# Two-layer diffusion trunk on one core: an opening without GpSimd custom instructions, window sums by shifted adds, six slots for the first modulation, and a first MLP begun by two tiles and two chunks

## The chip, the cores and the metric

One NeuronCore of a Trainium2 chip. The metric is the device time of one execution in microseconds (us). The engines are PE (TensorE), DVE (VectorE), ACT (ScalarE), POOL (GpSimd) and SP (SyncE), which issues most of the transfers from HBM.

## The reference

One stream of 512 tokens with 1024 features goes through two layers. Each layer is a token mixer and a squared-ReLU MLP, both in RMSNorm before and after, with shift, scale and gate from the conditioning vector `c`. The context stream is not needed for the result at this depth.

```python
silu_c = silu(c)
for i in range(2):
    sh_m, sc_m, gt_m, sh_f, sc_f, gt_f = split(silu_c @ ada_w[i] + ada_b[i], 6)   # 1024 -> 6 x 1024
    h = rms_norm(x, norm_g[i, 0]) * (1 + sc_m) + sh_m
    y = pool_mixer(h, pool_w, pool_scale) if i == 0 else short_conv_mixer(h, conv_in_w, conv_w, conv_out_w)
    x = x + gt_m * rms_norm(y, norm_g[i, 1])
    hf = rms_norm(x, norm_g[i, 2]) * (1 + sc_f) + sh_f
    x = x + gt_f * rms_norm(square(relu(hf @ ffn_w1[i])) @ ffn_w2[i], norm_g[i, 3])
```

`pool_mixer` has four groups of 256 features with windows of 2, 4, 8 and 16 tokens: mean over the window (cut at both ends of the sequence, divided by the true count) less the token itself, times a 256x256 matrix, times `pool_scale`. The conv mixer is 1024 to 3072, a gated convolution over 3 tokens, and 1024 to 1024. The MLP is 1024 to 4096 to 1024.

## The kernel before

Every large product is made of three float32r products of split operands: `w_hi` and `w_lo`, `in_hi` and `in_lo` (or `mid_hi`, `mid_lo`), in `three`, L347 to L350. Weights come in units of 1 MiB (2048 columns on 128 partitions). SP loads unit u into one of two `raw` slots, ACT makes `w_hi` (`split_hi`, L698), DVE makes `w_lo` (`split_lo`, L952), each in one of three slots. A unit is 48 products of 512 columns. Unit 0 holds the pool weights, units 1 to 32 the first MLP, 33 to 48 the conv mixer, 49 to 80 the second MLP. Two units form a pair that fills four PSUM banks; four pairs form a quarter of an MLP, two of them up (`feat_pair`), two down (`tok_pair`).

There is no scheduler. Each engine has its own list of instructions, written out by hand, runs it in order, and waits on semaphores. So whatever stands in an engine's list behind a waiting instruction waits too.

The first modulation (twenty chunks of 256 columns, `PRE`) is computed on PE. `load_pre` (L268) brings a chunk of 1 MiB into one of four slots; it waits until `add_up` has used the slot's last chunk. `add_up` (L509) multiplies it with silu(c) in eight products that share the array in four column groups, each with 32 output rows. `copy_sums` (ACT, L808) copies the partial sums, `turn_up` (PE, L523) adds the four groups and turns them into columns (scale, shift) or into a wide row (gate), and `columns` (DVE, L1129) reads them. Chunks 0 to 7 are scale and shift of the mixer, 8 to 11 its gate, 12 to 19 scale and shift of the MLP.

The opening: ACT and DVE normalize x, PE turns it into features (`turn_x`), ACT copies it to `xn_fm`. Windows of 2 and 4 are made by adds of GpSimd (L1352 to L1362), windows of 8 and 16 by band matrices on PE (`window`, L548), whose tables GpSimd builds with selects. ACT scales the window sums (`mean`, L818), DVE the tokens (`pool_input`), GpSimd subtracts (L1366), ACT and DVE split. `pool_group` (L567) multiplies a group, `group_squares` (ACT) and `group_out` (DVE) read the result, `group_gate` (DVE) applies the gate. `first_x` and `first_norm` (DVE, L1178, L1184) and `first_root` (ACT, L839) make the new x and its norm, a token tile of 128 at a time; `turn_first` (PE, L579), `copy_first` (ACT), `first_input`, `first_hi` and `first_lo` make the input of the MLP, a feature chunk of 128 at a time after all tiles. `start_pairs` (L591) holds the MLP's units 1 to 4, with the chunks 14 to 19 between its products.

Seven later rows of modulation (`LATER_SEGS`) are computed beside the products: DVE adds 56 pieces (`add_ada`, L964), then GpSimd reduces over the partitions (L1405), fetches and broadcasts a norm row (L1342), and DVE finishes (`finish_row`, L1054). The rows are used at two boundaries (`boundary`), between first MLP and conv mixer and between that and the second MLP.

## Time and profile before

| | us |
|---|---|
| median of three runs | 1044.35 (1042.13 to 1045.39) |
| profiled execution, device time | 1042.69 |
| its span in the profile | 1040.9 |
| PE busy | 968.6 (93%) |
| DVE busy | 540.8 (52%) |
| ACT busy | 339.6 (33%) |
| POOL busy | 88.6 (9%) |

Busy time is what an engine's instructions last, and products overlap, so a PE that is busy all the time still has a rate: 0.226 us from one product of 512 columns to the next at full clock. In the timeline a row is one instruction or a run of equal ones; the bracket says how long its engine stood idle before it and on what.

### The profile page before, as it was taken

The numbers are of one execution on the slowest core, as the hardware profiler recorded it, in microseconds if no ns is written. First come the engines' busy times: TensorE is split into PE (matmuls) and PEld (weight loads), VectorE is DVE, ScalarE is ACT, GpSimd is POOL, SyncE is SP. The second block draws the span as 40 slices with busy tenths as digits, with TensorE's granted clock in tenths as the row PEclk, the third lists the DMA queues.
The fourth block names the chain that finished last, engine by engine and source line by source line (L and its number), as shares of the span: only waits on it lengthen the run. The fifth ranks groups of instructions, "written<-read, shape, count | busy, mean of one in ns | idle before, by whom it ended". The sixth has DMA issues, their size and how long they took to land.

```text
span 1040.9 us, 11368 instructions
## 1 busy us (share of the span) xinstructions
PE 968.6 (93%) x4737; PEld 802.0 (77%) x4737; DVE 540.8 (52%) x582; ACT 339.6 (33%) x454; POOL 88.6 (9%) x65
## 2 busy tenths in 40 slices
PE   4685799999999999997999999889999999999997
PEld 3563568888888888887888887688888888888886
DVE  3345247455545645466576766646546433423444
ACT  5345134224214313333333223415213313312332
POOL 2520010003002100200002302000003000000000
PEclk9788889999999999998999999989999999999999
DMA  9547345344353442311555562035342232232301
GB/s 315 172 162 254 109 159 214 134 152 152 124 177 123 144 160 81 120 43 63 184 196 193 200 216 82 6 122 189 129 135 99 90 119 84 82 120 81 119 13 71
DMA packets 78813, 140.29 MB, mean 135 GB/s; under 512 B 3424, under 2 KB 33192, under 8 KB 78763
## 3 DMA queue, kind: packets, MB, share of 16 engines
q1 hardware_dynamic: 78240, 139.48, 39.7%
q8 instruction: 37, 0.61, 0.2%
q14 instruction: 14, 0.11, 0.0%
q0 software_dynamic: 384, 0.05, 0.0%
q10 hardware_dynamic: 138, 0.05, 0.0%
HBM read 137.47 MB, written 2.10 MB: 134 GB/s over the span
## 4 chain that ended last, share of the span: by engine, by line
PE 87%; DVE 3%; ACT 2%; issue 2%; DVEq 0%; ACTq 0%
PE ps L348 28%; PE ps L350 28%; PE ps L349 28%; PE ps L519 1%; ACT w_hi L704 1%; DVE w_lo L954 1%; PE ps L437 1%; ACT work L843 0%; ACT work L836 0%; PE ps L588 0%; PE ps L536 0%; DVE y L1014 0%; DVE in_lo L1025 0%; ACT work L741 0%; ACT in_hi L748 0%
## 5 line engine op out<-in xcount | busy, mean ns | idle before, releaser
L954 DVE TENSOR_TENSOR w_lo<-raw,w_hi 128x2048 fp32r<-128x2048 f32 x81 | 188.3, 2325 | 262.3 <-ACT w_hi L704 262.3
L348 PE MATMUL ps<-in_hi,w_hi 128*128 128x512 f32 (+1 forms) x768 | 292.6, 381 | 29.2 <-DVE in_lo L1199 12.8
L349 PE MATMUL ps<-in_lo,w_hi 128*128 128x512 f32 (+1 forms) x768 | 290.1, 378 | 0.0
L350 PE MATMUL ps<-in_hi,w_lo 128*128 128x512 f32 (+1 forms) x768 | 289.9, 377 | 0.0
L704 ACT ACTIVATE w_hi<-raw 128x2048 fp32r<-128x2048 f32 x81 | 154.6, 1910 | 381.9 <-PE ps L350 381.9
L348 PE MATMUL ps<-w_hi,mid_hi 128*128 128x512 f32 x576 | 224.5, 390 | 1.6 <-DVE w_lo L954 1.6
L350 PE MATMUL ps<-w_hi,mid_lo 128*128 128x512 f32 x576 | 224.1, 389 | 0.0
L349 PE MATMUL ps<-w_lo,mid_hi 128*128 128x512 f32 x576 | 224.1, 389 | 0.0
L348 PEld LDWEIGHTS ps<-in_hi,w_hi 128*128 128x128 f32 x768 | 148.9, 194 | 58.7 <-issue 17.3
L350 PEld LDWEIGHTS ps<-in_hi,w_lo 128*128 128x128 f32 x768 | 148.9, 194 | 25.5
L349 PEld LDWEIGHTS ps<-in_lo,w_hi 128*128 128x128 f32 x768 | 149.2, 194 | 24.8
L348 PEld LDWEIGHTS ps<-w_hi,mid_hi 128*128 128x128 f32 x576 | 108.1, 188 | 24.2 <-DVE w_lo L954 2.1
L350 PEld LDWEIGHTS ps<-w_hi,mid_lo 128*128 128x128 f32 x576 | 108.1, 188 | 22.5
L349 PEld LDWEIGHTS ps<-w_lo,mid_hi 128*128 128x128 f32 x576 | 108.1, 188 | 22.3
L964 DVE SCALAR_TENSOR_TENSOR ada_sum<-ada_raw,silu_t,ada_sum 128x1024 f32<-128x1024 f32 x56 | 74.9, 1338 | 1.3
L972 DVE TENSOR_TENSOR work<-work 128x512 f32<-128x512 f32 x64 | 44.1, 689 | 38.1 <-ACT mid_hi L715 37.8
L713 ACT ACTIVATE work<-ps 128x512 f32<-128x512 f32 x64 | 38.2, 598 | 75.9 <-DVE mid_lo L974 39.3
L983 DVE TENSOR_TENSOR y<-y,ps 128x512 f32<-128x512 f32 x48 | 32.2, 684 | 47.0 <-PE ps L350 47.0
L974 DVE TENSOR_TENSOR mid_lo<-work,mid_hi 128x512 fp32r<-128x512 f32 x64 | 49.3, 771 | 2.2
L1405 POOL PARTITION_ALL_REDUCE gate_row<-ada_sum x3 | 18.7, 6240 | 363.7 <-DVE ada_sum L964 363.7
L1405 POOL PARTITION_ALL_REDUCE mod_rows<-ada_sum x4 | 24.5, 6114 | 219.4 <-DVE ada_sum L964 219.4
L715 ACT ACTIVATE mid_hi<-work 128x512 fp32r<-128x512 f32 x64 | 40.5, 632 | 2.0
(137 smaller groups left out, 512.0 us busy)
## 6 DMA issues: line engine op xcount, KB each, us to landing
raw<-in_ffn_w_dram SPq DMA_DIRECT2D x64, 1024.0 KB, 5.2
ada_raw<-in_ada_w_dram SPq DMA_DIRECT2D x56, 512.0 KB, 5.6
raw<-in_conv_in_w_dram SPq DMA_DIRECT2D x16, 512.0 KB, 5.1
ada_raw<-in_ada_w_dram SPq DMA_DIRECT2D x6, 1024.0 KB, 6.0
ada_sum<-in_ada_w_dram SPq DMA_DIRECT2D x6, 1024.0 KB, 6.3
mod_rows<-in_ada_w_dram SPq DMA_DIRECT2D x5, 1024.0 KB, 7.8
raw<-in_conv_in_w_dram SPq DMA_DIRECT2D x4, 1024.0 KB, 5.9
raw<-in_conv_out_w_dram SPq DMA_DIRECT2D x4, 1024.0 KB, 6.0
```

Of the source, the lines that this page charges most:

```text
L348: nc.tensor.matmul(o, hi, b_hi, start=start, stop=False)
L349: nc.tensor.matmul(o, hi, b_lo, start=False, stop=False)
L350: return nc.tensor.matmul(o, lo, b_hi, start=False, stop=stop)
L704: nc.scalar.activation(w_hi[:, u % W_SLOTS, :], raw[:, u % RAW_SLOTS, :], ACT.Copy).then_inc(w_hi_ready, 1)
L713: nc.scalar.activation(work[:, n % 2, :], bank(p, m), ACT.Relu).then_inc(relu_done, 1)
L715: nc.scalar.activation(mid_hi[:, n, :], work[:, n % 2, :], ACT.Square).then_inc(hid_hi, 1)
L954: nc.vector.tensor_tensor(w_lo[:, u % W_SLOTS, :], raw[:, u % RAW_SLOTS, :], w_hi[:, u % W_SLOTS, :].bitcast(F32), ALU.subtract).then_inc( ...
L964: nc.vector.scalar_tensor_tensor(out=ada_sum[:, s % 2, :], in0=ada_raw[:, i % ADA_SLOTS, :], scalar=silu_t[:, 3, k:k + 1], in1=ada_sum[:, ...
L972: nc.vector.tensor_tensor(work[:, n % 2, :], work[:, n % 2, :], work[:, n % 2, :], ALU.mult).then_inc(hid_sq, 1)
L974: nc.vector.tensor_tensor(mid_lo[:, n, :], work[:, n % 2, :], mid_hi[:, n, :].bitcast(F32), ALU.subtract).then_inc(hid_lo, 1)
L983: nc.vector.tensor_tensor(y_tok[:, t, half(h)], y_tok[:, t, half(h)], bank(p, t), ALU.add).then_inc(y_sum, 1)
L1405: nc.gpsimd.partition_all_reduce(to, ada_sum[:, s % 2, :], channels=P, reduce_op=bass.bass_isa.ReduceOp.add).then_inc(row_summed, 1)
```

## The change

It replaces the opening and the way of the seven rows. No custom instruction of GpSimd is left (`partition_broadcast`, `partition_all_reduce`).

- Pool scale and the norm row are spread over the partitions by a one-row product on PE (`spread`), and DVE copies them. The gate's bias enters `add_up` as a one-row product, and DVE's `gate_copy` multiplies the sums with the norm row, so `group_out` leaves; ACT copies the group behind its squares.
- Windows are shifted sums over a padded `xn_fm`: window 2 on DVE, windows 4, 8 and 16 on GpSimd, with a product for the cut ends. The bands leave PE, `mean` leaves ACT, `pool_input` moves to ACT, scaling and subtraction become one DVE instruction (`diff`).
- Chunks 0 and 1 get slots of their own in `y`, so six chunks are asked for at once. The pairs use banks 0, 1, 4, 5 and 2, 3, 6, 7. The load of unit 1 stands before those of chunks 12 to 19.
- GpSimd makes `w_lo` of units 1, 2 and 3.
- The MLP's input for chunks 0 to 3 is made in quarters of two tiles and two chunks, straight from PSUM; unit 1 is multiplied in these quarters, then half of unit 2, unit 3, the rest of unit 2, unit 4.
- A later row is summed by four products on PE between two units of a pair (`sum_row`), finished by DVE from PSUM, written to DRAM and read back to all partitions. Its pieces are added at units `LATER_AT`.

```diff
+PRE_SLOTS = [4, 5] + [(i - 2) % 4 if i < PRE_F else 1 + (i - PRE_F + 1) % 3 for i in range(2, len(PRE))]
+LATER_AT = [4 + i for i in range(24)] + [28, 28, 29, 29, 30, 30, 35, 35] + [36 + i // 2 for i in range(16)] + [52 + i for i in range(8)]
+ROW_AT = {LATER_AT[NC * s + NC - 1] + 1: s for s in range(len(LATER_SEGS))}
+BANKS = ((0, 1, 4, 5), (2, 3, 6, 7))
...
             load(POOL_U)
-            for i in range(2, PRE_F + 2):
+            for i in range(2, PRE_F):
                 load_pre(i)
-            for u in range(1, 4):
-                load(u)
-                load_pre(PRE_F + 2 * u)
-                load_pre(PRE_F + 2 * u + 1)
+            load(1)
+            for i in range(PRE_F, PRE_F + 4):
+                load_pre(i)
+            load(2)
+            for i in range(PRE_F + 4, PRE_F + 6):
+                load_pre(i)
+            load(3)
+            for i in range(PRE_F + 6, len(PRE)):
+                load_pre(i)
...
+            def sum_row(u, p, free):
+                s = ROW_AT[u]
+                pe.wait_ge(ada_used, NC * (s + 1))
+                free(3)
+                for j in range(4):
+                    mm = nc.tensor.matmul(bank(p + 1, 3)[32 * j:32 * (j + 1), 0:Q], ones[:, 0:32], ada_sum[:, s % 2, quarter(j)],
+                                          start=True, stop=True)
+                mm.then_inc(row_summed, 1)
...
                 last.then_inc(unit_done, 1)
                 need_weights(u + 1)
+                if u + 1 in ROW_AT:
+                    sum_row(u + 1, p, next_free)
...
+            def spread(row):
+                for e in range(2):
+                    mm = nc.tensor.matmul(ps[:, e, :], ones[0:1, :], row[0:1, half(e)], start=True, stop=True)
+                mm.then_inc(row_spread, 1)
...
+                turn_first(0, 0)
+                turn_first(0, 2)
+                turn_first(1, 0)
+                part(0, 0)
+                add_up(PRE_F + 2)
+                turn_first(0, 3)
+                add_up(PRE_F + 3)
+                turn_first(1, 2)
+                turn_up(PRE_F + 2)
+                turn_up(PRE_F + 3)
+                turn_first(0, 1)
+                turn_first(1, 3)
+                part(1, 0)
+                turn_first(1, 1)
+                add_up(PRE_F + 4)
+                part(0, 1)
+                turn_up(PRE_F + 4)
+                part(1, 1).then_inc(unit_done, 1)
+                add_up(PRE_F + 5)
+                pe.wait_ge(f_made, 4)
+                second_unit(2)
...
+            pe.wait_ge(ones_ready, 1)
+            pe.wait_ge(row_in, 16 * 3)
+            spread(pool_row)
+            pe.wait_ge(ident_ready, 1)
...
             for i in range(4):
                 add_up(i)
-                window(BAND_CHUNK + i)
                 turn_up(i)
-            add_up(4)
+            pe.wait_ge(row_wide, 2)
             need_weights(POOL_U)
-            pool_group(0)
...
+            for g in range(1, GROUPS):
+                add_up(2 * g + 2)
+                pool_group(g - 1)
+                turn_up(2 * g + 2)
+                add_up(2 * g + 3)
+                turn_up(2 * g + 3)
             pool_group(3)
+            for i in range(10, PRE_F + 2):
+                add_up(i)
+                turn_up(i)
...
+            def diff(n):
+                dve.wait_ge(pool_h, n + 1)
+                dve.wait_ge(mod_step, n // 2 + 1)
...
+                nc.vector.scalar_tensor_tensor(out=win[:, n, :], in0=win[:, n, :], scalar=A_BY_W[:, n:n + 1], in1=xn_in[:, n, :],
+                                               op0=ALU.mult, op1=ALU.subtract).then_inc(pool_diff, 1)
...
+            def add_windows(g):
+                w, n = WINDOWS[g], slice(2 * g, 2 * g + 2)
+                length = T + w - 2
+                at = PAD - w // 2
+                nc.gpsimd.tensor_tensor(sums[0][:, :, 0:length], xn_fm[:, n, at:at + length], xn_fm[:, n, at + 1:at + 1 + length], ALU.add).then_inc(pairs_read, 1)
+                pool.wait_ge(pairs_read, g)
+                shift, level = 2, 0
+                while shift < w:
...
+                    nc.gpsimd.tensor_tensor(o, src[:, :, 0:length], src[:, :, shift:shift + length], ALU.add).then_inc(sum_step, 1)
...
+            for u in (1, 2, 3):
+                pool.wait_ge(w_hi_ready, u + 1)
+                pool.wait_ge(w_lo_ready, u)
+                nc.gpsimd.tensor_tensor(w_lo[:, u % W_SLOTS, :], raw[:, u % RAW_SLOTS, :], w_hi[:, u % W_SLOTS, :].bitcast(F32), ALU.subtract).then_inc(w_lo_ready, 1)
...
-                nc.gpsimd.partition_all_reduce(to, ada_sum[:, s % 2, :], channels=P, reduce_op=bass.bass_isa.ReduceOp.add).then_inc(row_summed, 1)
...
+                pool.wait_ge(row_made, s + 1)
+                pool.dma_start(rows_dram[s].rearrange("(j n) -> j n", j=4), fin[0:P:32, :]).then_inc(row_out, 16)
```

On ACT, `split_hi(1)` now stands before `first_root(0)`, `split_hi(2)` behind `first_hi(3)`, `split_hi(3)` behind `copy_sums(18)`. On DVE the columns of chunk 12 stand before `first_norm(0)`, those of chunk 13 before `first_x(3)`.

## Rows read from the trace of the kernel before

**Rows 1.** Stretches: bounds, length, PE, PEld, DVE, ACT, POOL busy, PEclk, DMA share, GB/s

```profile
106.10:171.50 65.40, 58.68 (x296) 44.46 (x297) 29.50 (x41) 22.80 (x30) 3.81 (x6) 0.90 0.42 142
171.50:474.00 302.50, 302.50 (x1340) 250.57 (x1339) 159.78 (x152) 89.53 (x101) 26.93 (x13) 1.00 0.38 130
...
96.00:102.00 6.00, 2.85 (x32) 1.94 (x30) 1.13 (x4) 4.54 (x6) 0.00 (x0) 1.00 1.03 358
```

**Rows 2.** Timeline of PE: start, duration, line, operation, and idle before it

```profile
42.16 1.01 PE L536 MATMUL ps<-picks,cu 128*128 128x1 f32 x4 [6.31 <-ACT cu L812]
...
48.55 0.58 PE L348 MATMUL ps<-w_hi,in_hi 128*128 128x256 f32 x1 [3.52 <-DVE w_lo L954]
...
53.83 0.75 PE L536 MATMUL ps<-picks,cu 128*128 128x1 f32 x4
...
56.09 0.61 PE L536 MATMUL ps<-picks,cu 128*128 128x1 f32 x4 [0.50 <-ACT cu L812]
56.56 0.36 PE L348 MATMUL ps<-w_hi,in_hi 128*128 128x256 f32 x1
...
59.60 1.07 PE L519 MATMUL ps<-ada_sum,cu 128*32 128x256 f32 x16
...
71.15 0.69 PE L533 MATMUL ps<-gate_row,ones 1*128 1x256 f32 x2
...
106.14 0.77 PE L348 MATMUL ps<-in_hi,w_hi 128*128 128x512 f32 x1 [6.17 <-DVE in_lo L1199]
...
119.42 0.79 PE L348 MATMUL ps<-in_hi,w_hi 128*128 128x512 f32 x1 [4.19 <-DVE in_lo L1199]
...
171.52 0.39 PE L348 MATMUL ps<-w_hi,mid_hi 128*128 128x512 f32 x1
...
641.58 0.50 PE L348 MATMUL ps<-w_hi,mid_hi 128*128 128x512 f32 x1 [1.64 <-DVE w_lo L954]
```

**Rows 3.** Timeline of POOL

```profile
13.12 0.28 POOL L1327 TENSOR_SCALAR_AFFINE_SELECT ident<-ident 128x128 f32<-128x128 f32 x1 [11.26 <-issue]
...
22.59 1.30 POOL L1342 PARTITION_BROADCAST pool_row<-pool_row  x1 [7.12 <-issue]
...
32.79 1.88 POOL L1352 TENSOR_TENSOR win<-xn_fm 128x1022 f32<-128x1022 f32 x1 [7.71 <-issue]
...
46.95 3.92 POOL L1366 TENSOR_TENSOR win<-win,xn_fm 128x512 f32<-128x512 f32 x2 [3.73 <-ACT win L826]
...
634.85 6.11 POOL L1405 PARTITION_ALL_REDUCE mod_rows<-ada_sum  x1 [35.47 <-DVE ada_sum L964]
```

**Rows 4.** Timeline of DVE

```profile
24.01 3.14 DVE L1205 TENSOR_TENSOR raw<-raw,pool_row 128x1024 f32<-128x1024 f32 x2 [4.40 <-POOL pool_row L1342]
...
85.21 2.48 DVE L1181 SCALAR_TENSOR_TENSOR xs<-y,st,xs 128x1024 f32<-128x1024 f32 x2
...
636.55 4.98 DVE L954 TENSOR_TENSOR w_lo<-raw,w_hi 128x2048 fp32r<-128x2048 f32 x1 [1.80 <-ACT w_hi L704]
```

**Rows 5.** Timeline of ACT

```profile
44.27 1.90 ACT L704 ACTIVATE w_hi<-raw 128x2048 fp32r<-128x2048 f32 x1
...
91.05 1.02 ACT L850 ACTIVATE xn_tok<-ps 128x1024 f32<-128x1024 f32 x1 [1.68 <-PE ps L588]
```

**Rows 6.** Chain that ended last, one piece: start, duration, what

```profile
71.50 1.46 ACT work L836 x8
```

**Rows 7.** Costliest groups of the page: count, busy, mean ns of one, idle before

```profile
L954 DVE TENSOR_TENSOR w_lo<-raw,w_hi 128x2048 fp32r<-128x2048 f32 x81 | 188.3, 2325 | 262.3 <-ACT w_hi L704 262.3
...
L964 DVE SCALAR_TENSOR_TENSOR ada_sum<-ada_raw,silu_t,ada_sum 128x1024 f32<-128x1024 f32 x56 | 74.9, 1338 | 1.3
```

**Rows 8.** DMA issues of the page: count, KB each, median us to landing

```profile
ada_sum<-in_ada_w_dram SPq DMA_DIRECT2D x6, 1024.0 KB, 6.3
mod_rows<-in_ada_w_dram SPq DMA_DIRECT2D x5, 1024.0 KB, 7.8
```

More of the change, by code:

```diff
@@ L600, in products @@
-                def products(u, k, m, chunk, start, stop):
-                    pe.wait_ge(f_lo, chunk + 1)
-                    o = feat_products(u, k, m, 0 if u in (1, 3) else 1, chunk, COLS, ALL, start, stop)
-                    if (u, k, m) in later:
-                        later[u, k, m]()
-                    return o
-                add_up(PRE_F + 2)
-                need_weights(1)
-                for k in range(UK):
-                    for m in range(4):
-                        last = products(1, k, m, k, k == 0, False)
@@ L612, in start_pairs, with part @@
[L612 to L622 removed]
+                def part(side, pair):
+                    pe.wait_ge(f_lo, FIRST_MADE.index((side, pair)) + 1)
+                    need_weights(1)
+                    for k in (2 * pair, 2 * pair + 1):
+                        for m in range(4):
+                            last = feat_products(1, k, m, 0, k, COLS, toks(2 * side, 2), k == 0 and side == 0, False)
+                    return last
@@ L623, in start_pairs @@
                 pe.wait_ge(cols_read, cols_value(len(PRE) - 1))
-                for k in range(UK):
-                    for m in range(2, 4):
-                        last = products(2, k, m, k, k == 0, False)
-                last.then_inc(unit_done, 1)
+                second_unit(0)
+                second_unit(1).then_inc(unit_done, 1)
                 need_weights(4)
@@ L882, in _ @@
             copy_sums(7)
-            mean(6)
-            mean(7)
-            copy_sums(8)
+            pool_input(6)
+            pool_input(7)
             diff_hi(6)
@@ new lines, in _ @@
+            nc.gpsimd.memset(xn_fm[:, :, 0:PAD], 0.0)
+            nc.gpsimd.memset(xn_fm[:, :, PAD + T:], 0.0).then_inc(pads_ready, 1)
+            for g in range(1, GROUPS):
+                for at, tokens in edges(g):
+                    for i, (_, count) in enumerate(tokens):
+                        op = nc.gpsimd.memset(edge[:, at + i:at + i + 1], WINDOWS[g] / count)
+            op.then_inc(edge_ready, 1)
+            pool.wait_ge(xn_copied, NT)
+            pool.wait_ge(pads_ready, 1)
```

572 lines of the change are left out of this document (265 added, 307 removed).

## The prediction

> **What bounds the kernel now.** I began with the busy shares by slice: PE is at 9 tenths nearly everywhere and falls only in the first four slices and at two later places. The table of stretches [rows 1] shows it in numbers. From 171.5 to 474 us PE is busy 302.5 of 302.5 us at full clock, one product each 0.226 us, so nothing that this change does to other engines can shorten that stretch. Before it the last stretch of the opening, 106.1 to 171.5, has PE busy 58.7 of 65.4 us at 0.90 of the clock. So I take the opening as a chain, see where each link waits, and rebuild the chain with the new orders. The end of it is one event: the first product of the MLP's second half, at 171.52 us [rows 2]; behind it the code of the PE stream is the same but for seven small sums. The change is worth what this event moves, less what the later part gains or loses.
>
> **Where the opening waits today.** GpSimd switches what it can run: it stands 11.26 us before the first select, 7.12 before the first broadcast, 7.71 before the first add of a window [rows 3]. The last add is done at 39.7; ACT has `mean(0)` in its queue ahead of `copy_sums(3)`, so PE stands 6.31 us at 42.16 [rows 2]; then w_hi and w_lo of the pool weights, and the first pool product comes at 48.55 [rows 2]. The pool stage then needs 36.7 us to `first_x(0)` at 85.21 [rows 4], the way from there to the MLP's first product 20.9 us (to 106.14), and the first four MLP units 65.4 us.
>
> **Step A, to the first pool product: 48.55 becomes 37.** The select at 13.12 and so the transposes at 13.63 stay. xn of tile 1 is now ready before ident, so the four turns run with only ACT's copies (1.0 us each, as the copy of a tile in [rows 5]) between them, and the features are complete at about 20.3 instead of 22.0. The spread of a row by PE is new: 256 columns of such a one-row product take 0.69 us at 71.15 [rows 2], so the four pieces of a row make at most 2.8, and I take 2.5, as they overlap; the first lies under the wait for ident, the second ends at 21.3. The 7.12 and 7.71 us before a broadcast and after it I take as gone with the broadcast; between 0 and 7.7 us may still stand before the adds, and the cover below hides either. The DVE then has: row copy 1.2 and two-window add 1.3 (nearest: 1.24 for 1024 elements, 2.48 for two [rows 4]), `columns` 0.5 twice, which come at 25.7 because the chunks follow each other each 2.1 us (add_up 1.07 at 59.60, ACT's copy 0.50 and turn_up 0.61 at 56.09 [rows 2]); the pool weights 3.1 (L1205 [rows 4]) to 28.8; two diffs 1.4 (half of 1.24 each and a little); ACT's hi, hi and w_hi, at 1.90 for 2048 elements [rows 5] 0.6+0.6+1.9, to 32.8; w_lo 2.3 [rows 7] to 35.1; add_up(4), 1.07 or cold 1.93, to about 37. Gain 11.5. The window sums on GpSimd: an add costs 1.88 us for 1022 elements [rows 3], there are 2+3+4 of these and five short ones of about 0.2, so 18.7 us from 20.5: group 1 is ready at 25 and needed at 37, group 2 at 31.5 and needed at 48, group 3 at 40 and needed at 56. That is the cover that hides a switch or a slow GpSimd.
>
> **Step B, pool stage: 36.7 becomes 34.5.** Four pool groups: the first cold 5.3 (48.55 to 53.83 [rows 2]), three warm at 3.0 (24 products; 56.56 to 59.60) = 14.3. Three plain add_ups 3.2, four with the bias product 1.07+0.35 = 5.7; eight turn_ups 5.0; the bias product is half of the 0.69 at 71.15, being in one of four column groups (bounds 0 and 0.69, 1.4 either way); ACT copies that nothing covers, five at 0.5 = 2.5; twice ACT's squares and the new copy of the group (1.46 [rows 6] and 1.02 [rows 5]) stand ahead of the sum copy, 1.1 each = 2.2; last gate product 1.2, at the same rate, and a short reciprocal on DVE = 1.4. Sum 34.3, so `first_x(0)` starts at about 71.5 instead of 85.2. The copy and the squares lie on ACT beside PE's next group; in the group where ACT is late they cost the 1.1 counted. One to three more cold groups would cost 2.3 each (5.3 less 3.0).
>
> **Step C, to the first MLP product: 20.9 becomes 13.8.** DMA is what counts: load(1) is issued once add_up(10) is done, 66.2, ahead of the slots of chunks 12 and 13. A loaded queue moves 358 GB/s [rows 1], 2.93 us for 1 MiB; the first lands after 5.7, for the 6.3 of [rows 8] held some queueing: 71.9, 74.9, 77.8. add_up(13), copy, turn_up, `columns` (1.1+0.5+0.6+0.4) bring DVE to 80.4; first_x(3) 1.28; ACT's squares and root 1.5; first_norm(3) 0.9; one turn 0.6, first_lo(0) 0.75. Together 85.3, against 106.14. `first_input(0)`, `first_norm(2)` and w_hi of unit 1 lie beside. Unit 1's w_lo is now GpSimd's: 2048 elements at 1.84 ns are 3.8 us, done at 77.6; cover until 85.
>
> **Step D, the first four units: 65.4 becomes 61.6.** Unit 1 in halves, 96 products of 256 columns at 0.12, the spacing in a warm pool group [rows 2], = 11.5; units 2 to 4, 144 at 0.2265 = 32.6; six add_ups 6.4; six turn_ups 3.0; five turns of the first tiles 3.0; half clock at the start 1.4 (the first product after a stall takes 0.77 or 0.79 instead of 0.39 [rows 2], and a few more like it); a bare copy 0.5; unit 2's w_lo late by 1.1 and unit 3's by 2.1, because ACT's w_hi comes only behind `first_hi(3)` and `copy_sums(18)` and GpSimd needs 3.8 where DVE needs 2.3. Sum 61.6: PE reaches the MLP's second half at 146.9. Today's stretch holds 43.5 us of products, 9.5 of chunks and 12 of waits; of the waits, 4.19 at 119.42 [rows 2] and a smaller one go, because two tiles and two chunks are ready while the rest is made. The opening gains 24.6.
>
> **Step E, the seven later rows.** GpSimd's reduce (6.11 us [rows 3]) and broadcast leave; PE gets four products of 256 columns. The eight of an add_up take 1.07 us [rows 2], so about 0.55 each row, 3.9 us in all; bounds 0.3 and 1.1 each, 2 to 8. It waits for `ada_used`. At the start of unit u (odd, second last of a pair) DVE still has about 2.1 us of hidden work, ACT 1.3 and then w_hi 1.9, then DVE w_lo 2.3 and one ada product 1.34 [rows 7] or two: done 6.9 to 8.3 us on, while the sum stands 10.9 us on (48 x 0.2265). So the margin is 2.6 to 4 us and the wait costs nothing; without it, the products of the pair's second unit would stand behind it. The round trip through DRAM has more than ten microseconds of cover, as the row is wanted units later. DVE's finish shrinks, off the path.
>
> **Step F, the second boundary.** The reduce at 634.85 runs to 640.96, and beside it w_lo takes DVE 4.98 us instead of 2.3 [rows 3, 4, 7]; PE stands 1.64 us behind it at 641.58 [rows 2]. That wait goes: -1.6. The boundary's other waits are chains of ACT and DVE that no edit touches. Ada products beside steps 28 to 30 delay the first boundary by nothing: DVE waits there for the second product group in any case.
>
> **A rule that speaks against it.** Beside DVE's two-operand work GpSimd's two adds of 512 took 3.92 us, alone 0.94 each would be 1.9 [rows 3]. The Trainium skill, "GPSIMD Engine Reference", section Key points, says that GpSimd shares its SBUF interfaces with VectorE and that an instruction of DVE with two SBUF inputs contends with it; by that rule the trace agrees, and what it does here is rival 1. The same page, section 3.1, gives 4.5 us for an add of 2048 elements and calls DVE twice as fast; no add of that length is in the trace, my 3.8 is scaled from 1022 elements, and by the page's figure unit 2 and unit 3 would each come 0.7 us later, 1022 becoming 1023.4.
>
> **The sum.** 1042.69 - 24.6 + 3.9 - 1.6 = 1020.4 for an execution like the profiled one (span 1040.9 and 1.8 around it). The median of the three runs shown is 1.7 above it, so 1022.
>
> **Rivals.** (1) GpSimd becomes the bound. With the factor 2.1 of [rows 3] the window sums last 39 us, end at 60 and are needed at 56, +4; the w_lo of units 2 and 3 come 4.1 later each; with one more cold group about 14: 1036. For it: DVE is busy over half of the opening. Against: DVE idles just where units 2 and 3 are split. Chance 0.14. (2) The loads come later than reckoned: 1 MiB took 6.3 us in the median from issue to landing in one slot and 7.8 in another [rows 8], and load(1) is put before chunks 12 and 13. If these overlap badly, chunk 13 lands at 86 instead of 77.8, +8: 1030. For it: the queue of 12 MiB behind 66 us; against: 358 GB/s were held over whole stretches. Chance 0.12. (3) Better than reckoned: no cold group, the waits in D all covered, 5.3 less 3.0, 1.4 and 3.2: 1015. Chance 0.10. (4) Slower: PE now waits in its own stream for DVE's ada products. If these stand one unit (10.9 us) further back in DVE's queue than I count, each sum waits 10.9 less a margin of 2.6 to 4, so about 7.5 us seven times, 53 us, against a gain of 22: 1075. It decides from 3.2 us a row on. Against: DVE is busy 53% from 171.5 to 474. Chance 0.03. (5) The opening isn't shorter, since its chain is bound by something I don't see, as ACT's order, and only E and F remain: 1042.69 + 3.9 - 1.6 + 1.7 = 1047. Chance 0.03.
>
> **Chances and range.** The forecast itself has 0.58, with 1017 to 1028 as its own range. From 1013 to 1036 it reaches into rivals 1 to 3 and holds 0.8 or a little more. Faster by over 0.3% (3 us, about what a measurement tells from nothing) is the forecast with rivals 1 to 3, 0.94; same 0.02; slower 0.04.
>
> **What would show it.** First pool product near 37, `first_x(0)` near 71.5, first MLP product near 85, the MLP's second half near 147. GpSimd's adds start at about 20.5 with no long idle. Its w_lo of 2048 takes 3.8 us; 8 would be rival 1. No PE wait at the seven sums. It is wrong if PE's second half of the MLP starts later than 158 or if products between 147 and 450 show waits.

## The result, and the profile after

The changed kernel takes 1035.26 us (median of 4 runs, 1034.93 to 1036.25) against 1044.43 before (median of 4): a ratio of 0.9917 [0.9899, 0.9934], so 9.2 us faster. The forecast was 1022. The profiled execution took 1035.34 us with a span of 1033.6.

PE is busy 970.5 us, GpSimd 69.2 instead of 88.6. The page of the kernel after, the lines by slices (25.8 us each, busy share in tenths, PEclk the granted clock):

```profile
PE 970.5 (94%) x4769; PEld 797.7 (77%) x4769; DVE 538.7 (52%) x563; ACT 339.8 (33%) x448; POOL 69.2 (7%) x103
PE   6486999999999999997999999799999999999997
PEclk9596999999999999998999999989999999999999
```

The second slice (25.8 to 51.7 us) still has PE at 4 tenths; there the forecast failed. The timeline of PE after, with the milestones that answer to [rows 2] (start, duration, operation, idle before it and its cause):

```profile
8.66 3.75 PE L595 MATMUL ps<-pool_row,ones 1*128 1x512 f32 x4 [8.66 <-DMA gate_row<-in_ada_b_dram]
...
37.57 1.02 PE L589 MATMUL ps<-picks,cu 128*128 128x1 f32 x4 [6.54 <-ACT cu L870]
...
45.98 1.93 PE L574 MATMUL ps<-ada_sum,cu 128*32 128x256 f32 x16 [7.40 <-issue]
47.84 0.58 PE L380 MATMUL ps<-w_parts,in_hi 128*128 128x256 f32 x1
...
84.93 1.93 PE L574 MATMUL ps<-ada_sum,cu 128*32 128x256 f32 x16 [4.49 <-DMA ada_sum<-in_ada_w_dram]
...
96.61 0.56 PE L380 MATMUL ps<-in_hi,w_parts 128*128 128x256 f32 x1
...
131.30 0.70 PE L380 MATMUL ps<-in_hi,w_parts 128*128 128x512 f32 x1 [2.74 <-POOL w_parts L1425]
...
160.25 0.39 PE L380 MATMUL ps<-w_parts,mid_hi 128*128 128x512 f32 x1
...
236.18 0.39 PE L382 MATMUL ps<-in_hi,w_parts 128*128 128x512 f32 x1
236.50 0.64 PE L409 MATMUL ps<-ada_sum,ones 128*32 128x256 f32 x8
237.07 0.50 PE L380 MATMUL ps<-in_hi,w_parts 128*128 128x512 f32 x1
...
237.63 0.39 PE L382 MATMUL ps<-in_hi,w_parts 128*128 128x512 f32 x1
```

| milestone | before [rows 2, 4] | forecast | after |
|---|---|---|---|
| first pool product | 48.55 | 37 | 47.84 |
| `first_x(0)` starts on DVE | 85.21 | 71.5 | 81.83 |
| first MLP product | 106.14 | 85.3 | 96.61 |
| MLP's second half | 171.52 | 146.9 | 160.25 |
| from there to the end of the span | 869.4 | 871.7 | 873.3 |

Of the 13.4 us by which 160.25 misses 146.9, 10.8 are there at the first pool product. The two rows 37.57 and 45.98 show where: PE stands 6.54 us on ACT's copy of a chunk and then 7.40 for which the profile names nothing ("issue"). In the kernel the wait for the split pool weights (`need_weights(POOL_U)`) stands right ahead of this chunk, and DVE's `w_lo` (41.46, 4.42 us) ends at 45.88; so this wait, too, is for DVE. ACT in its turn waits for DVE. The table of stretches says who is busy (length, PE, PEld, DVE, ACT, POOL, granted clock, share of DMA, GB/s):

```profile
20.00:46.00 26.00, 10.41 (x87) 5.33 (x86) 24.39 (x18) 6.63 (x10) 24.70 (x15) 0.61 0.65 208
46.00:82.00 36.00, 29.78 (x256) 21.17 (x256) 16.44 (x32) 20.01 (x54) 0.14 (x1) 0.90 0.48 158
```

In the 26 us before the first pool product DVE is busy 24.4 and GpSimd 24.7. Neither has that much to do: in the second experiment below DVE's same operations from the pool weights to `w_lo` take 8.6 us instead of 19.9. The two timelines after, first GpSimd's:

```profile
20.59 1.90 POOL L1403 TENSOR_TENSOR sums<-xn_fm 128x1028 f32<-128x1028 f32 x1 [17.97 <-ACT xn_fm L863]
22.57 2.93 POOL L1410 TENSOR_TENSOR win<-sums 128x1024 f32<-128x1024 f32 x1
...
27.88 2.77 POOL L1410 TENSOR_TENSOR sums<-sums 128x1032 f32<-128x1032 f32 x1
...
36.73 4.26 POOL L1410 TENSOR_TENSOR sums<-sums 128x1048 f32<-128x1048 f32 x2
...
113.31 4.61 POOL L1425 TENSOR_TENSOR w_parts<-raw,w_parts 128x2048 fp32r<-128x2048 f32 x1 [24.61 <-ACT w_parts L761]
```

and DVE's:

```profile
21.40 1.23 DVE L1159 COPY ada_raw<-ps 128x1024 f32<-128x1024 f32 x1 [4.42 <-PE ps L595]
22.54 1.22 DVE L1176 TENSOR_TENSOR win<-xn_fm 128x1024 f32<-128x1024 f32 x1
23.79 1.74 DVE L1178 TENSOR_SCALAR win<-win 128x2 f32<-128x2 f32 x1
...
25.62 0.17 DVE L1197 SCALAR_TENSOR_TENSOR mod<-mod,vec 128x2 f32<-128x2 f32 x1
...
26.01 5.72 DVE L1271 TENSOR_TENSOR raw<-raw,pool_row 128x1024 f32<-128x1024 f32 x2
31.65 3.04 DVE L1211 SCALAR_TENSOR_TENSOR win<-win,mod,xn_fm 128x512 f32<-128x512 f32 x2
...
34.80 1.87 DVE L1197 SCALAR_TENSOR_TENSOR mod<-mod,vec 128x2 f32<-128x2 f32 x1
...
36.78 4.75 DVE L1216 SCALAR_TENSOR_TENSOR in_lo<-win,mod,in_hi 128x512 fp32r<-128x512 f32 x2
41.46 4.42 DVE L1003 TENSOR_TENSOR w_parts<-raw,w_parts 128x2048 fp32r<-128x2048 f32 x1
...
115.13 2.81 DVE L1197 SCALAR_TENSOR_TENSOR mod<-mod,vec 128x2 f32<-128x2 f32 x1
```

An operation of DVE on 2 elements (L1178) takes 1.74 us here; one like it at 25.62 takes 0.17. It starts at 23.79 and is over at 25.53, when GpSimd's add that began at 22.57 is over (25.50). L1197 at 115.13, again 2 elements, lasts 2.81 us, to 117.94; GpSimd's `w_lo` beside it runs from 113.31 to 117.92. In the other direction, GpSimd's add at 22.57 took 2.93 us instead of 1.90: DVE's two-window add had begun at 22.54 and was over at 23.76. So the reading is that an instruction that one of the two has begun keeps the other out to its end. DVE's copy out of PSUM at 21.40 took 1.23 beside an add that kept its 1.90, so an operation that reads from PSUM alone isn't held. The reading is made on GpSimd's adds and subtractions. Beside the custom reduce of the kernel before (634.85 to 640.96, [rows 3]) `w_lo` was over at 641.53 [rows 4], only 0.57 us behind it and with 2.29 of its own, so there it wasn't kept out to the end.

Work held in DVE from 26 to 46 us, each less its time alone (2.36, 1.41, 0.16, 1.41 and 2.29 in the rows of the second experiment): 3.36 + 1.63 + 1.71 + 3.34 + 2.13 = 12.2 us. DVE has no idle time between these rows, and PE's chunk and first pool product follow them. (In the second experiment, where the hold-up is gone from here, DVE waits 0.80 us for ACT instead, and 11.4 of the 12.2 are won.)

The Trainium skill, "SBUF — State Buffer", section Who interferes with whom, describes just this: the port pair that VectorE and GpSimd share is locked for a whole instruction and not split, against an instruction of VectorE with two SBUF inputs, or one in a two-port mode, and the one that issues later blocks. The ends that coincide (117.94 and 117.92) agree with it. The prediction drew only on the short sentence of the GpSimd page.

The effect stood in the trace of the kernel before as well. An operation on 2 elements like the one that takes 0.16 at 27.25 there took 1.05 beside GpSimd's two subtractions (40.73, 2.49 us for two). DVE's timeline before:

```profile
40.96 1.05 DVE L1146 SCALAR_TENSOR_TENSOR mod<-mod,vec 128x2 f32<-128x2 f32 x1
```

### The profile page after: what moved, and what is told of

It reads as the page before. It is cut to its first block, busy times and chain, and to the rows that moved or that the text cites. A ratio compares the mean times of both kernels' runs of the same rounds, so it can differ in the third digit from the quotient of the medians.

```text
span 1033.6 us, 11447 instructions
## 1 busy us (share of the span) xinstructions
PE 970.5 (94%) x4769; PEld 797.7 (77%) x4769; DVE 538.7 (52%) x563; ACT 339.8 (33%) x448; POOL 69.2 (7%) x103
## 3 DMA queue, kind: packets, MB, share of 16 engines
HBM read 141.77 MB, written 2.13 MB: 139 GB/s over the span
## 4 chain that ended last, share of the span: by engine, by line
PE 88%; DVE 2%; ACT 1%; issue 1%; DMA 1%; POOL 0%; DVEq 0%; SPq 0%; ACTq 0%
PE ps L380 29%; PE ps L381 28%; PE ps L382 28%; PE ps L574 1%; DMA ada_sum<-in_ada_w_dram 1%; PE ps L488 1%; ACT w_parts L761 1%; POOL w_parts L1425 0%; PE ps L589 0%; PE ps L409 0%; PE ps L632 0%; DVE xn_tok L1257 0%; DVE y L1063 0%; DVE in_lo L1074 0%; ACT work L798 0%
## 5 line engine op out<-in xcount | busy, mean ns | idle before, releaser
L1003 DVE TENSOR_TENSOR w_parts<-raw,w_parts 128x2048 fp32r<-128x2048 f32 x78 | 180.8, 2320 | 265.6 <-ACT w_parts L761 265.5
L380 PE MATMUL ps<-in_hi,w_parts 128*128 128x512 f32 (+1 forms) x784 | 295.3, 377 | 19.7 <-issue 7.8
L381 PE MATMUL ps<-in_lo,w_parts 128*128 128x512 f32 (+1 forms) x784 | 292.8, 373 | 0.0
L382 PE MATMUL ps<-in_hi,w_parts 128*128 128x512 f32 (+1 forms) x784 | 292.5, 373 | 0.0
L761 ACT ACTIVATE w_parts<-raw 128x2048 fp32r<-128x2048 f32 x81 | 154.6, 1910 | 391.4 <-PE ps L382 389.8
L380 PE MATMUL ps<-w_parts,mid_hi 128*128 128x512 f32 x576 | 224.4, 390 | 0.0
L382 PE MATMUL ps<-w_parts,mid_lo 128*128 128x512 f32 x576 | 224.1, 389 | 0.0
L381 PE MATMUL ps<-w_parts,mid_hi 128*128 128x512 f32 x576 | 224.1, 389 | 0.0
L380 PEld LDWEIGHTS ps<-in_hi,w_parts 128*128 128x128 f32 x784 | 152.3, 194 | 49.9 <-issue 12.3
L382 PEld LDWEIGHTS ps<-in_hi,w_parts 128*128 128x128 f32 x784 | 152.3, 194 | 24.6
L381 PEld LDWEIGHTS ps<-in_lo,w_parts 128*128 128x128 f32 x784 | 152.5, 195 | 24.1
L380 PEld LDWEIGHTS ps<-w_parts,mid_hi 128*128 128x128 f32 x576 | 108.1, 188 | 22.4
L382 PEld LDWEIGHTS ps<-w_parts,mid_lo 128*128 128x128 f32 x576 | 108.1, 188 | 22.4
L381 PEld LDWEIGHTS ps<-w_parts,mid_hi 128*128 128x128 f32 x576 | 108.1, 188 | 22.3
L1021 DVE TENSOR_TENSOR work<-work 128x512 f32<-128x512 f32 x64 | 44.1, 689 | 45.6 <-ACT mid_hi L772 45.4
L589 PEld LDWEIGHTS ps<-picks,cu 128*128 128x128 f32 x64 | 10.1, 223 | 18.7 <-ACT cu L870 18.5
```

The lines of the kernel that those rows point to most:

```text
L380: nc.tensor.matmul(o, hi, b_hi, start=start, stop=False)
L381: nc.tensor.matmul(o, hi, b_lo, start=False, stop=False)
L382: return nc.tensor.matmul(o, lo, b_hi, start=False, stop=stop)
L761: nc.scalar.activation(w_hi[:, u % W_SLOTS, :], raw[:, u % RAW_SLOTS, :], ACT.Copy).then_inc(w_hi_ready, 1)
L1003: nc.vector.tensor_tensor(w_lo[:, u % W_SLOTS, :], raw[:, u % RAW_SLOTS, :], w_hi[:, u % W_SLOTS, :].bitcast(F32), ALU.subtract).then_inc( ...
L1021: nc.vector.tensor_tensor(work[:, n % 2, :], work[:, n % 2, :], work[:, n % 2, :], ALU.mult).then_inc(hid_sq, 1)
```

## The experiments

Theory 1 is that the hold-up of DVE and GpSimd eats the gain of the opening. Its rivals are the order of PE's and DVE's work (the spread of the rows ahead of the turns) and the loads. All runs stood beside runs of the kernel before, whose medians were 1043.57 to 1043.90 us (1044.43 beside the kernel after). So a difference of 1 us between a run here and the kernel after means nothing by itself, and the ratios to before are the better measure.

One more rival is the rate of PE, which differs between executions (last experiment). It does not explain step A: in the traces of after, e1, e2 and e9 the first spread takes the same 3.75 us, `add_up(0)` starts at 21.29, 21.04, 21.23 and 20.81, and of the five chunks up to the first pool product the first takes 1.07 us and the last three 1.93 in all four (1.94 in e9), the second 1.07 or, in e1, 1.63.

**e1: GpSimd's sums nearly empty.** One full add for each group stays; the window sums of 4, 8 and 16 are not computed.

```diff
-                    o = win[:, n, :] if 2 * shift == w else sums[(level + 1) % 2][:, :, 0:length]
-                    nc.gpsimd.tensor_tensor(o, src[:, :, 0:length], src[:, :, shift:shift + length], ALU.add).then_inc(sum_step, 1)
+                    nc.gpsimd.tensor_tensor(sums[(level + 1) % 2][:, :, 0:2], src[:, :, 0:2], src[:, :, shift:shift + 2], ALU.add).then_inc(sum_step, 1)
```

> Changed kernel, but GpSimd makes one full add per window group (3 of 1.9 us) and tiny ones else, so the window sums of 4, 8 and 16 tokens are left out of the computation. Theory 1 (GpSimd's adds and DVE's work between 20 and 46 us hold each other up; DVE took 5.72 us for the pool weights where it took 3.14 before, 4.75 for two diff_lo where 1.41 is seen later, 4.42 for w_lo where 2.29): DVE's instructions fall back to 2.45, 1.4 and 2.3 once the adds end at about 27, the first pool product comes at 38 to 40 instead of 47.8, first_x(0) at 72 to 75 instead of 81.8, the kernel takes 1025 to 1028 us. Theory 2 (the chain is bound by the landing of chunk 4 or by ACT's order): the first pool product stays at 47 to 48 and the time at 1035.

Measured: 1026.66 us (1026.13 to 1027.76), ratio 0.9838 [0.9821, 0.9854], first pool product at 37.98. Theory 1 had 38 to 40 and 1025 to 1028. The hold-up isn't wholly gone: one full add for each group is left, and DVE's `in_lo` at 30.69 took 3.12 us instead of 1.41. GpSimd's timeline of this kernel has the effect at its purest:

```profile
20.35 0.29 POOL L1403 TENSOR_TENSOR sums<-xn_fm 128x64 f32<-128x64 f32 x1 [17.73 <-ACT xn_fm L863]
...
26.73 2.20 POOL L1411 TENSOR_TENSOR sums<-sums 128x4 f32<-128x4 f32 x2
```

A sum of 64 elements took 0.29 us, and two sums of 4 elements took 2.20: they lie beside DVE's product of the pool weights (26.40, 2.47 us for two).

**e2: all the work, but two groups' sums behind the split of the pool weights.** The result is whole.

```diff
             for g in range(1, GROUPS):
+                if g == 2:
+                    pool.wait_ge(w_lo_ready, 1)
                 add_windows(g)
```

> Changed kernel with all its work; GpSimd only waits for w_lo of the pool weights before it begins windows 8 and 16. Theory 1: after about 26 us DVE is alone, w_lo is ready at about 37, the first pool product at 38 to 40; then windows 8 and 16 run from 37 to about 55 beside the first two pool groups, in DVE's idle time, and are needed at about 46 and 56; part of the gain may be given back there. Time 1025 to 1030 us. Theory 2: first pool product at 47 to 48, and window 8 then late besides, so 1035 to 1040.

Measured: 1032.37 us (1028.42 to 1033.07), ratio 0.9883 [0.9863, 0.9904]; first pool product at 36.48, `first_x(0)` at 74.89. DVE's timeline of this kernel shows its operations alone, and then the hold-up again where the sums now lie:

```profile
25.95 2.36 DVE L1271 TENSOR_TENSOR raw<-raw,pool_row 128x1024 f32<-128x1024 f32 x2
28.23 1.41 DVE L1211 SCALAR_TENSOR_TENSOR win<-win,mod,xn_fm 128x512 f32<-128x512 f32 x2
...
29.74 0.16 DVE L1197 SCALAR_TENSOR_TENSOR mod<-mod,vec 128x2 f32<-128x2 f32 x1
...
30.02 1.41 DVE L1216 SCALAR_TENSOR_TENSOR in_lo<-win,mod,in_hi 128x512 fp32r<-128x512 f32 x2
32.23 2.29 DVE L1003 TENSOR_TENSOR w_parts<-raw,w_parts 128x2048 fp32r<-128x2048 f32 x1 [0.80 <-ACT w_parts L761]
...
35.52 3.85 DVE L1211 SCALAR_TENSOR_TENSOR win<-win,mod,xn_fm 128x512 f32<-128x512 f32 x2 [0.93 <-ACT xn_fm L881]
...
41.61 1.88 DVE L1201 TENSOR_SCALAR mod<-mod 128x2 f32<-128x2 f32 x1
```

The first five rows are the times alone; 35.52 and 41.61 are held (3.85 and 1.88 us instead of 1.41 and, for 2 elements, 0.17), now behind the first pool product. 11.4 us are won there and 6.9 at `first_x(0)`: 4.5 go back in the pool stage, where PE now waits for DVE's `in_lo` (1.27 us at 46.53) and longer for ACT (2.81 at 55.08 instead of 1.51). The first product came earlier than theory 1 had it (38 to 40), the median time later (1025 to 1030). The traced execution, 1028.42, is the fastest; the other three took 1032.27 to 1033.07, so by the median only 2.9 us are gained on after, and where those three lost 4 us isn't traced.

**e9: the same adds, each in two halves.** The diff shows the first add of a group; the others are halved likewise. The same bytes, so a shared bandwidth would change nothing; a lock for whole instructions would.

```diff
-                nc.gpsimd.tensor_tensor(sums[0][:, :, 0:length], xn_fm[:, n, at:at + length], xn_fm[:, n, at + 1:at + 1 + length], ALU.add).then_inc(pairs_read, 1)
+                for e in (0, 1):
+                    op = nc.gpsimd.tensor_tensor(sums[0][:, e, 0:length], xn_fm[:, 2 * g + e, at:at + length], xn_fm[:, 2 * g + e, at + 1:at + 1 + length], ALU.add)
+                op.then_inc(pairs_read, 1)
```

> The changed kernel with each of GpSimd's full adds (1.9 us for 2 x 512) issued as two adds of 512, the same work in all. The ends of DVE's slowed operations fall on the ends of GpSimd's adds (DVE on 2 elements: 115.13 + 2.81 = 117.94, GpSimd's w_lo: 113.31 + 4.61 = 117.92). Theory A, the two engines exclude each other by whole instructions: an operation of DVE that reads its operands from SBUF waits for the end of the instruction that GpSimd has begun, and the reverse. Then each of DVE's eight held operations between 26 and 46 us waits for one half add, some 0.95 us instead of 1.5 to 1.9: 5 to 6 us of the 12 go, the first pool product moves from 47.84 to 42 to 43.5, the time to 1030 to 1032 if GpSimd's later end costs nothing. Theory B, they share bandwidth, each at half speed while both work: the same bytes, the first pool product stays at 47 to 48.5 and the time at 1035 to 1036.5.

Measured: 1030.14 us (1027.83 to 1030.61), ratio 0.9864 [0.9844, 0.9884], first pool product at 39.75. DVE's timeline of this kernel:

```profile
23.31 0.89 DVE L1178 TENSOR_SCALAR win<-win 128x2 f32<-128x2 f32 x1
...
25.40 3.25 DVE L1271 TENSOR_TENSOR raw<-raw,pool_row 128x1024 f32<-128x1024 f32 x2
...
31.66 0.82 DVE L1197 SCALAR_TENSOR_TENSOR mod<-mod,vec 128x2 f32<-128x2 f32 x1
...
35.50 2.28 DVE L1003 TENSOR_TENSOR w_parts<-raw,w_parts 128x2048 fp32r<-128x2048 f32 x1
```

2 elements take 0.89 and 0.82 us instead of 1.74 and 1.87, the weights 3.25 instead of 5.72, the split 2.28 instead of 4.42. Theory B falls: 5.1 us of the median for no work less. The product came even earlier than the 42 to 43.5 of theory A. Not each operation gained alike: held over their time alone, the weights are 0.89 us, the two diffs 1.57 (2.98 in all, hardly less than the 3.04 after), the 2 elements 0.66, `in_lo` 1.57 (2.98), and the split not at all: GpSimd then had only its two short operations for the cut ends of the windows (35.11, 2.73 us for two on 8 elements), and they waited for the split. Together 4.7 us instead of 12.2, so 7.5 of the 8.1; another 0.5 is the earlier start (`add_up(0)` at 20.81).

**e4: PE turns the first two tiles before it spreads the pool's scale.**

```diff
-            pe.wait_ge(row_in, 16 * 3)
-            spread(pool_row)
...
             for j in range(NT):
+                if j == 2:
+                    pe.wait_ge(row_in, 16 * 3)
+                    spread(pool_row)
                 turn_x(j)
...
             norm_x(0)
-            row_on_all(0, pool_row[:, :])
...
             norm_x(3)
+            row_on_all(0, pool_row[:, :])
```

DVE's copy of the spread row goes behind its four tiles with it.

> Changed kernel, but PE turns tiles 0 and 1 before it spreads the pool scale. PE stood until 8.7 us for the row's transfer and then needed 3.75 us at half clock, while xn of tile 0 was ready at 9.3 and ident at 1.6. Theory A: features complete near 17 instead of 20.5, the whole opening moves by 2.5 to 3.5 us, time 1032. Rival B (the start is bound by the transfers of x and the first chunks): under 1 us, 1034.5 to 1035.5.

Measured: 1033.44 us (1032.15 to 1038.27), ratio 0.9912 [0.9891, 0.9932]; `add_up(0)` at 18.37 (after: 21.29), first pool product at 44.93. The spread at 8.66 in the timeline after was a cost of 2 to 3 us that step A had put under a wait for `ident`; `ident` was there at 1.6 us. The traced execution is 2.6 us ahead at the MLP's second half (157.67); the median falls by 1.8, between the two theories, and by the ratios it isn't told from after.

**e3: the loads of chunks 12 and 13 ahead of unit 1's.**

```diff
-            for i in range(2, PRE_F):
+            for i in range(2, PRE_F + 2):
                 load_pre(i)
             load(1)
-            for i in range(PRE_F, PRE_F + 4):
+            for i in range(PRE_F + 2, PRE_F + 4):
```

> Changed kernel, but the loads of chunks 12 and 13 are asked for before that of unit 1. Theory A (PE stands 4.5 us at add_up(12) and works at half clock after it, since chunk 12 is queued behind unit 1, whose load waits for add_up(10)): the wait goes, add_up(12) starts near 80.5 instead of 84.9, first MLP product near 92 instead of 96.9, time 1030 to 1032. Rival B (the wait is only moved: unit 1 lands later, its w_lo on GpSimd becomes the last): first MLP product at 95 to 97, time 1034 to 1036.

Measured: 1035.64 us (1034.58 to 1036.96), ratio 0.9921 [0.9906, 0.9936]; the first MLP product at 96.66 against 96.61. PE's timeline, then ACT's, of this kernel:

```profile
85.48 1.01 PE L589 MATMUL ps<-picks,cu 128*128 128x1 f32 x4 [3.75 <-ACT cu L870]
```

```profile
81.88 1.91 ACT L761 ACTIVATE w_parts<-raw 128x2048 fp32r<-128x2048 f32 x1 [1.30 <-DMA raw<-in_ffn_w_dram]
...
85.06 0.36 ACT L870 ACTIVATE cu<-ps 128x256 f32<-128x256 f32 x1
```

The wait of 4.49 us for the load (84.93 after) became 3.75 for ACT's copy of the chunk: in ACT's order the split of unit 1 (81.88) stands ahead of it, and that one now waits for its load. Product and time are where rival B put them, but not for its reason: the first MLP product has no wait before it, so `w_lo` of unit 1 wasn't the last.

**e5 and e6: e2 and e4 together, and then the loads with ACT's order mended.** e6 also has the loads of e3, and ACT's split of unit 1 stands behind the copy of chunk 12 and the root of tile 1:

```diff
-            split_hi(1)
             first_root(0)
             copy_sums(PRE_F)
             first_root(1)
+            split_hi(1)
```

> The two changes of e2 and e4 together: GpSimd's sums of windows 8 and 16 wait for the split of the pool weights, and PE turns the first two token tiles before it spreads the pool's scale. Theory A, the two act on different links of one chain (e2: DVE's work between add_up(0) and the first pool product; e4: the start of add_up(0)), so their gains add: add_up(0) at 18.4 us, first pool product at 33.5 to 34.5 (e2 had 36.48), and the time 2 to 3 us under e2's median of 1032.4, 1029.5 to 1030.5. Theory B, behind e2 another thing (the loads of chunks, the sums of windows 8 and 16 that now end at 52 us) sets the pace: first pool product earlier but first_x(0) at 74 to 75 as in e2, time 1031.5 to 1033.

> As e5, and the loads of chunks 12 and 13 ahead of the load of unit 1, with ACT's split of unit 1 behind the copies of chunk 12 and the root of tile 1, so that it no longer stands ahead of them. Theory A: the wait of 4.3 to 4.6 us for chunk 12 goes, and the split of unit 1 (ACT 1.9, GpSimd 4.5 after the load) is still in time: first MLP product 3 to 4 us nearer to first_x(0) than in e2 (14.6 there), 11 to 12, and the time 3 us under e5. Theory B: unit 1 becomes the last thing ready (its load now lands some 5 us later, at about 80, and 6.4 us of splitting follow), the wait is at the first MLP product instead and the time is within 1 us of e5.

Measured: e5 1028.56 us (1025.21 to 1037.38), ratio 0.9868 [0.9833, 0.9903], first pool product at 33.41 and `first_x(0)` at 71.78, so up to there theory A: the gains add. The runs are 12 us apart, so the median can't tell its 1029.5 to 1030.5 from the 1031.5 to 1033 of theory B. e6 1032.51 us (1026.14 to 1037.64), ratio 0.9896 [0.9871, 0.9921]: no gain, and neither theory's picture. In e6 the turn of chunk 12 still waited 3.50 us for ACT's copy and the next turns 3.91 for DVE. From `first_x(0)` to the first MLP product it is 14.7 us in e5 and 16.2 in e6, where theory A had 11 to 12; which one thing sets this stretch is not settled.

**e7: `w_lo` of units 2 and 3 on DVE again.**

```diff
-            for u in (1, 2, 3):
+            for u in (1,):
                 pool.wait_ge(w_hi_ready, u + 1)
...
             first_lo(3)
+            split_lo(2)
...
             first_lo(4)
+            split_lo(3)
```

> The w_lo of units 2 and 3 on DVE (as before the change) instead of GpSimd; unit 1's stays on GpSimd. PE waited 2.74 us at 131.3 behind GpSimd's w_lo of unit 3, and beside GpSimd's two a DVE operation on 2 elements took 2.81 instead of 0.16 us. Theory A, that wait is worth its length: MLP's second half 2.5 to 3 us earlier (157.5), time 1032.3 to 1033. Theory B, DVE's own chain (first_input, first_lo) slips by its 2.3 us and PE waits there instead: time 1035 to 1036.

Measured: 1032.25 us (1031.86 to 1032.56), ratio 0.9888 [0.9872, 0.9904]. PE's timeline of this kernel:

```profile
129.21 0.50 PE L380 MATMUL ps<-in_hi,w_parts 128*128 128x512 f32 x1 [0.49 <-DVE w_parts L1003]
```

Where PE stood 2.74 us (131.30 after) it stands 0.49, and the median falls by 3.0. The MLP's second half begins at 156.54 instead of 160.25, from a first MLP product at nearly the same time (96.46, 96.61). Theory A.

**e8: each row sum twice.**

```diff
-                for j in range(4):
+                for j in (0, 1, 2, 3) * 2:
```

> The four products that sum a row over the partitions are issued twice, seven times in the kernel. The stream of PE shows a set as 0.64 us and the products behind it 0.77 us later than without. Theory A, the price is the products' own rate: seven more sets cost 7 x 0.64 to 0.77 = 4.5 to 5.4 us, 1039.7 to 1040.7. Theory B, most of it is a fixed cost of entering and leaving the four column groups: a second set adds 0.43 or less each, 3 us or less, 1036.5 to 1038.3.

Measured: 1038.87 us (1037.61 to 1039.56), ratio 0.9951 [0.9937, 0.9964]: 3.6 us more than after. PE's timeline of this kernel, the doubled set:

```profile
236.78 1.07 PE L409 MATMUL ps<-ada_sum,ones 128*32 128x256 f32 x16
237.78 0.50 PE L380 MATMUL ps<-in_hi,w_parts 128*128 128x512 f32 x1
```

A set is 0.64 us, two are 1.07: 0.43 for the products. In the stream after, 236.18 to 237.63 is 1.45 us where three steps of 0.227 make 0.68: 0.77 more. So 0.43 is products and 0.34 is paid once for a set. That it is the going in and out of the four column groups is not shown: PE's waits for `ada_used` and for the bank stand ahead of the first set alone, and could be it. Seven more sets at 0.43 are 3.0 of the measured 3.6; theory B is the nearer, by the stream (0.44 more from the product before the sum to the one after it, at each of the seven places) rather than by the time, whose interval reaches both theories.

**e10, e11, e12: the edits that gained, together.** e10 is e2 with e7, e11 is e5 with e7, e12 is e11 with GpSimd's adds in halves.

> e2 and e7 together: the sums of windows 8 and 16 behind the split of the pool weights, the w_lo of units 2 and 3 on DVE. They act on different stretches, so theory A adds them: e2's median 1032.4 less 3.0 = 1029.4. Theory B, in e7 the gain came from where the loads fell, and with the opening 6 us earlier they are late instead: 1031 to 1032.5. As for the spread of the runs: e2, e4 and e5 had runs 4 to 12 us apart and e7 within 0.7; if the early opening itself spreads them (loads racing the chain), e10 spreads by 4 us or more; if only the moved turns do (e4, e5), by 4 us at most as e2.

> e5 and e7 together, the three edits that each gained. Additive: e5's 1028.6 less 3.0 = 1025.6, the lowest run near 1022.2. Rival: DVE is the engine that ends last after e5, so its 4.6 us more of w_lo show: 1027 to 1029.

> e11 with GpSimd's adds in halves. Theory A (exclusion by whole instructions): DVE's operations beside the sums of windows 8 and 16, at 35 to 50 us, wait for halves; in e2 they took 3.85, 3.08 and 4.14 us instead of 1.4 and 1.88 instead of 0.17, so up to 4 us of 9 go, of which some lies under PE's products of a pool group: 1 to 3 us under e11. Theory B (shared bandwidth): as e11 within 1 us.

| | median us | runs | ratio to before |
|---|---|---|---|
| e10 | 1025.13 | 1020.49 to 1029.55 | 0.9815 [0.9788, 0.9842] |
| e11 | 1025.22 | 1022.00 to 1031.37 | 0.9827 [0.9791, 0.9864] |
| e12 | 1021.48 | 1018.32 to 1027.35 | 0.9792 [0.9763, 0.9821] |

e12, with the whole result, beats both kernels: 22.4 us under before and 13.8 under after. It is 3.7 us under e11, where theory A had 1 to 3, but the intervals of the two overlap and the traced e11 had the slower PE in its opening (below), so this doesn't count as a second proof beside e9. e11 came where the additive sum had it (1025.6). e10 came out 4.3 us under its additive 1029.4, below both of its theories, and is no slower than e11, which has one more gaining edit; so the gains aren't simply additive. The medians of these kernels are uncertain by some 3 us, for their runs spread by 9.

Why some of them spread, one comparison suggests. e5 and e11 have the same instructions up to the first pool product. PE's timeline of e5, then of e11:

```profile
12.44 1.98 PE L595 MATMUL ps<-pool_row,ones 1*128 1x512 f32 x4
...
18.15 1.07 PE L574 MATMUL ps<-y,cu 128*32 128x256 f32 x16
...
33.41 0.58 PE L380 MATMUL ps<-w_parts,in_hi 128*128 128x256 f32 x1
```

```profile
12.70 3.78 PE L595 MATMUL ps<-pool_row,ones 1*128 1x512 f32 x4
...
23.72 1.94 PE L574 MATMUL ps<-y,cu 128*32 128x256 f32 x16
...
41.21 0.58 PE L380 MATMUL ps<-w_parts,in_hi 128*128 128x256 f32 x1
```

The same spread takes 1.98 us in one and 3.78 in the other, the same chunk 1.07 and 1.94, and the first pool product differs by 7.8 us. The granted clock is given as 1.00 from 9 to 20 us in both; the rate of the products is what differs, by a factor of nearly two. From 20 to 33 us the record says 0.59 in e5 and 1.00 in e11, and yet a chunk takes 1.93 us in both (25.97 in e5, 27.11 in e11). So the clock on record can't be read before its first change; the length of a known row can. The kernel after, too, begins at the lower rate (3.75 for the spread at 8.66, 1.98 for the one at 19.38); in e11 it goes on to the first pool product. What decides isn't settled.

e11's runs fall in two heaps, 1022.0 to 1022.3 and 1028.2 (the profiled one) to 1031.4, with a mean clock on record of 0.968 to 0.969 in the first and 0.976 in the second: the slower have the higher one, as they would if they, too, had the lower rate under a clock given as 1.00. Of the slower three one is traced. It isn't the whole of the spread. e10, which leaves PE's turns where they were, spreads by 9 us as well, and there the higher clock goes with the shorter time (0.973 at 1020.49, 0.965 at 1029.55); its expectation had put 4 us or more down to the early opening itself.

## Why the prediction was wrong

It missed by 1035.34 less 1020.4, 14.9 us for an execution like the profiled one. Step by step:

- **Step A, 37 forecast, 47.84 measured (10.8 of the 14.9). This step failed.** Its terms for DVE, the pool weights 3.1, two diffs 1.4 and `w_lo` 2.3, took DVE's times without a GpSimd beside it, and the 18.7 us of adds on GpSimd were laid beside them, with a cover of 12 to 16 us. The cover held: neither PE nor DVE nor ACT has a row from 20 to 82 us that waits for GpSimd. But beside them DVE was held for 12.2 us, and DVE was the chain: from the columns to the end of `w_lo` 9.4 us were forecast (25.7 to 35.1) and 19.9 measured (26.01 to 45.88). e1 takes most of the adds away and gets 37.98; e2 moves them and gets 36.48 with all the work done; e9 halves their length and gets 39.75. Rival 1 had the contention and its factor [rows 3], but charged it to GpSimd alone, and so priced the wrong engine. The trace could have told: beside GpSimd's work `w_lo` took 4.98 instead of 2.3 us [rows 4, 7], which the prediction itself used in step F, and 2 elements took 1.05 (40.96 above).
- **Within step A**, the select and the start were too late (`ident` at 1.6 instead of 13.4, no 11.26 us wait at all) and the spread of the pool's scale too cheap (3.75 us, and 8.66 us of waiting for its row, where 2.5 and a cover were taken). The two errors cancelled by luck: `add_up(0)` came at 21.29, as forecast, and e4 shows 2.9 us to be had there.
- **Step B** 34.5 forecast, 34.0 measured.
- **Step C** 13.8 forecast, 14.8 measured. The loads were on time, so rival 2 did not come: chunk 12's products began 3.1 us after `first_x(0)` (forecast 3.4 for its landing), chunk 13's 6.5 after it (6.3). But PE stood 4.49 us before them, and its clock was low (0.59 in the row below): a chunk took 1.93 us and its turn 1.01 where the sum had 1.1 and 0.6. The table of stretches after:

```profile
80.00:100.00 20.00, 12.38 (x70) 8.81 (x70) 13.17 (x23) 10.16 (x19) 4.79 (x1) 0.59 1.02 334
```

- **Step D** 61.6 forecast, 63.6 measured. PE's waits came as forecast, 0.69, 0.51 and 2.74, 3.9 together against 3.2 and 0.5. The chunks and turns took 11.2 us instead of 12.4. What was short is the term for half clock, 1.4: the products of the four units took 48.5 us from start to start where 44.1 and this 1.4 were reckoned, 3.0 more, at a mean granted clock of 0.94 (the first of them 0.56 instead of 0.28 us). The wait of 2.74 is what e7 takes away, and with it some of the low clock: its products took 47.2. GpSimd's `w_lo` took 4.79, 4.61 and 4.50 us where 3.8 was reckoned from a shorter add. The Trainium skill, "GPSIMD Engine Reference", section 3.1, has 4.5 us for 2048 elements; the rows 113.31 and 126.74 (4.61 and 4.50) agree, and the page's figure would have been the better term, though it isn't what the step missed by.
- **Step E** 0.55 a row forecast, 0.77 measured (5.4 in seven instead of 3.9), with no wait for DVE at any of the sums, so rival 4 was rightly set aside. e8 parts the 0.77 in 0.43 of products and 0.34 once for a set.
- **Step F** right: no wait for `w_lo` after the second boundary is left, and its 4.98 us are 2.29.

Added: 10.8 - 0.5 + 1.0 + 2.0 + 1.5 = 14.8. Two numbers come near a forecast by luck. The measured 1035.3 lies within 1 us of rival 1's 1036 and inside the wide range that was drawn to it, but what rival 1 tells of did not happen: the window sums ended at 46.1 us and not at 60, and `w_lo` took 4.5 to 4.8 us and not 8. The prediction's own sign of being wrong, the MLP's second half later than 158, did (160.25). And e12 stands at 1021.48, near the forecast of 1022, but with gains that the forecast did not have (e4's order, e7's `w_lo`); e1, nearest to the opening without the hold-up, stands at 1026.66 with the MLP's second half at 151.10, 4.2 behind the forecast.

## What to carry to other kernels

Work put on GpSimd is free only if DVE, too, is off the path while it runs: where DVE is the chain, add GpSimd's instructions to DVE's time one by one (each held operation waits for up to the whole instruction that GpSimd has begun, were it for two elements; one that takes its data from PSUM did not wait). Put such work behind DVE's last link, or cut it in short instructions; both gained here without doing less (e2 2.9 us by the median and 6.9 in the traced execution, e9 5.1). And when an engine's row shows twice its time beside another's, price the slowing in both directions before calling anything hidden.
